# VectorE's order in the crossed groups of a two-layer decoder kernel: weight sums spread between combinations

## The reference

```
x = LN(alpha*x + 0.5 * (silu(x @ w_gate1) * (x @ w_up1)) @ w_down1)
x = LN(alpha*x + W_o(gated merge of three mixers: latent attention, short convolution, S5 scan))
x = LN(alpha*x + 0.5 * (silu(x @ w_gate2) * (x @ w_up2)) @ w_down2)
```

## Time and profile before

| | |
|---|---|
| median of three runs | 2623.1 us |
| the profiled execution | 2621.69 us |
| its span in the trace | 2619.9 us |
| TensorE busy | 2554.5 us, 98% |
| VectorE busy | 1483.3 us, 57% |
| ScalarE busy | 911.3 us, 35% |
| GpSimd busy | 1270.2 us, 48% |
| groups of part 1, layer 0 | 1044.9 to 1134.0 us of the span |
| groups of part 2, layer 0 | 1180.2 to 1265.9 us |
| groups of part 1, layer 1 | 2338.4 to 2427.6 us |
| groups of part 2, layer 1 | 2472.0 to 2557.0 us |

### The profile page before, as it was taken

How to read it: one execution, slowest core, us unless ns; L and a number is a source line. 1 busy time by engine, 2 the same in 40 slices (tenths; PEclk the granted TensorE clock), 3 DMA queues, 4 the chain that set the end, 5 groups by cost and what they waited for, 6 DMA issues and landing times.

```text
span 2619.9 us, 51230 instructions
## 1 busy us (share of the span) xinstructions
PE 2554.5 (98%) x20356; PEld 2427.1 (93%) x20356; DVE 1483.3 (57%) x2475; ACT 911.3 (35%) x1610; POOL 1270.2 (48%) x708
## 2 busy tenths in 40 slices
PE   9999999999999999999999999999999999999997
PEld 9999999998899999999999999999977788888897
DVE  6665444964443473737566554449644435848376
ACT  4222224235532242424352222242355322534343
POOL 4444435412244455959554444354132444769592
PEclk9999999999999999999999999999999999999999
DMA  5333324302223333333233333243122233333232
GB/s 162 99 88 89 88 81 106 81 24 62 61 77 94 97 81 89 98 96 108 71 111 96 88 89 88 81 106 81 26 64 66 77 96 93 97 97 107 77 96 76
DMA packets 457379, 226.99 MB, mean 87 GB/s; under 512 B 42384, under 2 KB 456336, under 8 KB 457200
## 3 DMA queue, kind: packets, MB, share of 16 engines
q1 hardware_dynamic: 450880, 217.09, 30.0%
q10 hardware_dynamic: 6320, 7.41, 1.0%
HBM read 220.20 MB, written 2.10 MB: 85 GB/s over the span
## 4 chain that ended last, share of the span: by engine, by line
PE 87%; DVE 6%; issue 3%; ACT 1%; POOL 1%; DMA 0%; ACTq 0%; SPq 0%; POOLq 0%; DVEq 0%
PE ps L687 59%; PE ps L821 14%; PE ps L797 4%; PE ps L710 3%; PE ps L1033 1%; PE ps L1118 1%; PE ps L1157 1%; POOL w_lo L602 1%; PE ps L1133 1%; PE ps L1122 1%; PE ps L1040 1%; DVE s_state L2162 1%; DVE stat L2133 0%; DVE ln_in L1795 0%; PE ps L1135 0%
## 5 line engine op out<-in xcount | busy, mean ns | idle before, releaser
L602 POOL TENSOR_TENSOR w_lo<-w_raw,w_hi 128x1024 fp32r<-128x1024 f32 (+4 forms) x400 | 859.3, 2155 | 1156.2 <-ACT w_hi L1276 1155.7
L1276 ACT ACTIVATE w_hi<-w_raw 128x1024 fp32r<-128x1024 f32 (+4 forms) x400 | 372.6, 936 | 635.5 <-PE ps L687 432.0
L687 PE MATMUL ps<-x_hi,w_hi 128*128 128x264 f32 (+2 forms) x2720 | 395.9, 296 | 4.3 <-ACT hid_rest L1276 3.6
L687 PE MATMUL ps<-x_hi,w_lo 128*128 128x264 f32 (+2 forms) x2720 | 388.5, 293 | 0.6 <-POOL w_lo L602 0.6
L687 PE MATMUL ps<-x_lo,w_hi 128*128 128x264 f32 (+2 forms) x2720 | 388.5, 293 | 0.0
L687 PEld LDWEIGHTS ps<-x_hi,w_hi 128*128 128x128 f32 x2720 | 355.2, 188 | 19.0 <-ACT hid_rest L1276 4.0
L687 PEld LDWEIGHTS ps<-x_hi,w_lo 128*128 128x128 f32 x2720 | 355.2, 188 | 11.0 <-POOL w_lo L602 1.3
L687 PEld LDWEIGHTS ps<-x_lo,w_hi 128*128 128x128 f32 x2720 | 355.3, 188 | 9.8
L1835 DVE TENSOR_TENSOR ps<-hid_rest,ps 128x528 f32<-128x528 f32 (+1 forms) x56 | 39.7, 710 | 241.0 <-PE ps L687 230.1
L602 POOL TENSOR_TENSOR w_lo<-w_sum,w_hi 128x512 fp32r<-128x512 f32 x90 | 138.4, 1547 | 52.0 <-ACT w_hi L1276 52.0
L602 POOL TENSOR_TENSOR w_lo<-w_pair,w_hi 128x512 fp32r<-128x512 f32 x108 | 155.1, 1450 | 9.7 <-ACT w_hi L1276 9.7
(11 more groups left out here) (345 smaller groups left out, 4460.2 us busy)
## 6 DMA issues: line engine op xcount, KB each, us to landing
w_raw<-in_w_in SPq DMA_DIRECT2D x82, 512.0 KB, 3.7
w_raw<-in_ffn_w_down SPq DMA_DIRECT2D x64, 512.0 KB, 4.1
w_raw<-in_ffn_w_up SPq DMA_DIRECT2D x56, 512.0 KB, 3.7
w_raw<-in_ffn_w_gate SPq DMA_DIRECT2D x48, 512.0 KB, 3.7
w_pair<-in_ffn_w_gate SPq DMA_DIRECT2D x40, 512.0 KB, 5.1
w_pair<-in_ffn_w_up SPq DMA_DIRECT2D x32, 512.0 KB, 5.1
w_raw<-in_ffn_w_down SPq DMA_DIRECT2D x32, 384.0 KB, 3.4
w_raw<-in_w_o SPq DMA_DIRECT2D x16, 512.0 KB, 4.1
```

The costliest lines, as they stand in the source:

```text
L602: pool.tensor_tensor(held(w_lo, c), src, held(w_hi, c).bitcast(f32), ALU.subtract).then_inc(w_split, 1)
L687: ins = nc.tensor.matmul(dst, wk, x[:, k0 + k, tokens], start=first and k == 0 and n == 0, stop=last and k == n_tiles - 1 and n == 2)
L1276: return nc.scalar.activation(out, in_, f, **kw)
```

## The change

```diff
                         if q:
                             make_hidden(part, f - 2)
-                        add_weights(m + 1)
+                            add_weights(m, (3,))
+                        add_weights(m + 1, (0, 1))
                         combine(gate, range(3))
                         if q:
                             rest_hidden(part, f - 2)
-                        combine(gate, range(3, 5))
+                        combine(gate, (3,))
+                        add_weights(m + 1, (2,))
+                        combine(gate, (4,))
+                        add_weights(m + 1, (3,))
+                        up_unit = (part, q, 1)
+                        if f < nf - 2:
+                            add_weights(m + 2, (0, 1))
+                            combine(up_unit, range(4))
+                            add_weights(m + 2, (2,))
+                            combine(up_unit, (4,))
+                            continue
+                        if part == len(PARTS) - 1:
+                            layer_norm_shift(sp)
+                        combine(up_unit)
+                        make_hidden(part, f)
+                        rest_hidden(part, f)
                         if m + 2 < N_CROSS:
                             add_weights(m + 2)
-                        else:
-                            layer_norm_shift(sp)
-                        combine((part, q, 1))
-                    if part:
-                        make_hidden(part, nf - 2)
-                        rest_hidden(part, nf - 2)
```

## The result

The changed kernel takes 2632.2 us (median of five runs, 2628.8 to 2633.5) against 2621.5 before (median of five runs too): ratio 1.0039, 95% interval 1.0024 to 1.0053. It is slower, by 10.7 us. Run again beside the experiments, on one chip with the kernel before, it gave 1.0035 (1.0024 to 1.0046), 2630.4 against 2622.1 us. The execution profiled here took 2628.8 us, with a span of 2627.0.

The account below looks back on a forecast made before the run. It took TensorE, busy 98% of the span, as the bound, so only its waits could be won: 25.3 us of gaps removed, 22.0 of new waits added, 3.3 less, giving 2619.8 us, range 2604 to 2630.

Parts of the forecast that it names:

- The old gaps: TensorE's 18 idle gaps in the crossed groups of layers 0 and 1, costing 25.3 us, would all go.
- The new wait before form 4: Gate units of q > 0: TensorE waits for ScalarE's copy, 1.65 us in layer 0, 2.02 in layer 1, six times each.
- the walk: Step-by-step timing of sums, roundings and splits from a gate unit's start, giving waits of 1.65 and 2.02 us.
- Groups in sum: Total loss in the crossed groups: 25.3 us before, 22.0 after, so 3.3 us less.
- rival (b): Groups of q > 0: late up pair makes sum 0 lose another round, 1.26 us per wait; 2634.9 us, chance 0.15.
- The 0.4 us of slack: Before sum 0 in groups of q > 0: margin left by the longest landing of the up pair's load.
- The down loads of q = 3 ... come 5.5 us later: I take nothing: Part 1's down loads, behind pair m+2 on SyncE's queue: no cost, at worst 1 us in two places.
- (a): GpSimd not backed up after the hidden work in gate units: 12 waits of 0.3 us, 2601.4 us, chance 0.15.
- (c): Groups bound by the loop of sum, rounding and split, not TensorE: time unchanged at 2623 us, chance 0.15.
- 0.19 on slower: Whole kernel: the chance of 0.19 given to a measured slowdown, beside faster 0.38 and same 0.43.

Follow-up runs that it names:

- h1: The changed kernel loading only an eighth of the second tile of each weight pair, so the output is wrong: 2627.5 us, ratio 1.0022.
- e1: The changed kernel with ScalarE's copy for form 4 moved ahead of its roundings in parts 1 and 2: 2614.1 us, ratio 0.9968.
- e2: The changed kernel with ScalarE rounding a part's third down chunk after the last hidden rounding, not before it: 2622.7 us, ratio 1.0001.
- k1: f with ScalarE making the copy five times in a row in gate units of q > 0: 2621.2 us, ratio 0.9996.
- e4: The changed kernel with its late sums made early, none left for the next group: 2605.1 us, ratio 0.9934.
- f: e4 with ScalarE rounding the third down chunk after the last hidden rounding: 2601.3 us, ratio 0.9921.
- g1: e4 with the gate unit's sums late again as in the change, the up unit's early: 2627.3 us, ratio 1.0025.
- f2: f with ScalarE's copy moved ahead of its roundings: 2605.7 us, ratio 0.9932.

## Why the prediction was wrong

It said 2619.8 us, no clear change most likely, with 2630 as the upper end. Measured were 2632.2 and, in the repeat, 2630.4. The steps one by one:

**The old gaps go: right.** None stands before form 5 in the changed kernel. I took 25.3 us for them. By start-to-start times they were 24.0, as a gap costs 0.17 us beyond its idle time and not the 0.25 I had. I had read a form as 1.455 us, but the two forms between 1085.26 and 1088.18 are 2.92, so 1.46 each, 20.44 for fourteen and 1.23 for the delay.

**The new wait before form 4: right in place, cause and size.** I walked to 1.65 us in layer 0 and 2.02 in layer 1. The trace has 1.58 and 1.94, GpSimd's pauses are 3.65 and 1.37 us where the walk had 3.9 and 1.4, and the stretches of layer 0 are 86.60 and 86.63 us, where 4 x 20.37 + 3 x 1.65 are 86.4. h1 and e1 confirm the cause. The Trainium skill's rule (SBUF — State Buffer, "SBUF: two separate sides") of a loser that blocks for the whole other instruction would have given some 0.3 us more in each. The contended sums here take 1.67 us as before, and the measurement decides for the walk's 0.55 us behind the split.

**Groups in sum.** Forecast 25.3 to 22.0. Measured 24.0 to 22.7 in the repeat, and 24.0 to 24.0 in the first profile, where late pairs are my rival (b) in part of the groups. The 0.4 us of slack is lost in four groups of each profile, not in none or all. Rival (b)'s point of decision, 7.1 us after issue, and its price, 1.26 us, were well placed: in the first profile the two groups whose sum 0 started 7.1 and 7.4 us after issue waited 1.25 and 1.23 us more than the others, and the two at 6.7 and 7.0 us at most 0.05 more.

**The step that failed: "The down loads of q = 3 ... come 5.5 us later: I take nothing".** I asked only when TensorE would need those chunks. The third one is needed late. But its rounding stands ahead of the last hidden rounding on ScalarE, which works in order, and TensorE needs that at once. Nor is it the queue behind pair m+2 that delays this chunk: its load is issued when GpSimd has split the first down chunk, 7.2 us before the end of part 1 in the kernel before and 1.4 us in the change (1126.56 and 1130.63). In part 2, which has no such pair, it is 4.2 and 1.0 us. I priced 1 us in two places for another reason. It is four places. From the windows of the second profile: 0.7 us in the first down stretch and 1.1 in that of layer 1; 1.4 in layer 0's downs and norm (80.23 against the 78.85 of e2, both at a clock of 0.98); and 1.7 behind the last groups, where TensorE's last instruction starts 55.9 us after them and 54.2 before. That is 4.9 us. e2 shows it directly.

**What the sum had no term for: TensorE's clock.** 0.9923 against 0.9936 on average is 0.13% of the time, an estimate of 3.4 us if TensorE sets the pace wherever the clock is low. In k1 a clock lower by 0.26% came with 3.5 us beyond the added delays, about half of that measure. In the groups it is more: in the windows above the four stretches of groups are 353.1 us in sum, 348.3 in the kernel before, though the delays are 1.3 us less. The other 6.1 us go with the lower clock of layer 1. Its part 2, forecast even or 1 us longer, is 6.4 us longer: 2.2 by delays (7.3 against 5.1), the rest with the clock. Over the whole execution most of this is balanced by other stretches: the mean clocks of the two executions are 0.993 and 0.994.

Together: delays in the groups -1.3 (repeat), ends +4.9, clock up to +3.4, so up to +7.0 us, and the medians of the repeat differ by 8.3, its interval being 6.3 to 12. What part of the rest belongs to late pairs in other executions is open.

**Rivals.** (a) did not occur in the change. Its mechanism was nevertheless the lever: put the late sums early and GpSimd isn't backed up (e4). (c) was wrong, the same loop ran at TensorE's pace in e4. None of my rivals held the part's end or the clock, and so 0.19 on slower was too low.

## What to carry to other kernels

When work of one engine is made later, follow the whole in-order program of each engine behind it, not only the consumer of the thing delayed: ask what else stands behind the instruction that now waits longer. A "free" delay of a load here cost 4.9 us, where the waits that the change was about came out even or 1.3 us better. Spreading work between others pays only if it also keeps the next engine fed; the order that gives the sums as early as they fit (e4) is 17 us faster than the kernel before and 25 us faster than the change.

## What the runs showed of the hardware

TensorE's granted clock has two levels here, 2.4 and 1.2 GHz; in the windows view they are 1.00 and 0.50. In the groups of layer 1 it averages 0.96 and 0.94 in the second profile of the change (0.98 and 0.96 in the first), 0.98 and 1.00 in the kernel before, and 1.00 in the early orders e4 and f. The second profile around its longest wait, and four windows in order of time:

```profile
2499.44 1.23 PE L821 MATMUL ps<-x_hi,w_hi 128*128 128x256 f32 x4 [3.02 <-ACT crossed_first L1276]
```
```profile
2496.42:2499.42 3.00, 0.00 (x0) 0.00 (x0) 2.10 (x2) 2.43 (x6) 3.00 (x2) 0.97 0.05 14
2499.44:2502.44 3.00, 3.00 (x14) 3.00 (x15) 2.56 (x5) 0.46 (x1) 2.72 (x3) 0.50 1.04 294
2503.00:2521.00 18.00, 18.00 (x153) 17.80 (x151) 13.67 (x17) 8.19 (x16) 14.93 (x10) 1.00 0.22 59
2523.15:2526.15 3.00, 3.00 (x17) 3.00 (x16) 2.23 (x5) 0.11 (x1) 3.00 (x3) 0.50 0.61 179
```

During the wait the clock is full (0.97), behind it half; it is full again for 18 us, and half behind the next wait, of 1.79 us. The traces of this case agree: the clock falls 22 times inside the groups, five times in this one, and each fall lies within 1.4 us of the end of a wait of 1.8 to 3.0 us. The waits of 1.42 us in layer 0 have no fall behind them.

k1 shows that waits alone are enough. But not each wait of that size does it: g1, with delays of 1.2 to 2.6 us before form 4, kept 0.9946 on average, and f2, whose waits are mostly of up to 1 us, had 0.9946 too. Which waits do it stays open.

In one stretch a low clock cost nothing. Layer 0's downs with the norm take 78.85 us at 0.98 in e2, with TensorE busy for 75.86, and the same in f at 1.00, busy for 74.86:

```profile
1256.66:1335.51 78.85, 74.86 (x623) 74.08 (x621) 49.22 (x103) 35.87 (x62) 35.20 (x22) 1.00 0.31 92
```
